# Routing and expert rows tile by tile in a two-block transformer kernel on one core

## The reference

```
for i in range(2):                       # second model
    h, hc = modulate(rmsnorm(x)), modulate(rmsnorm(xc))
    q, k, v = split(h @ w_qkv[i]); qc, kc, vc = split(hc @ w_qkv[i])
    x = x + gt_a * (attention @ w_o[i])          # xc likewise, in layer 0 only
    tokens = [modulate(rmsnorm(x)); modulate(rmsnorm(xc))]   # layer 1: x only
    # router: one of 4 groups, then the top 2 of its 8 experts
    y = sum over 2 experts of weight * (silu(t @ w_gate[e]) * (t @ w_up[e])) @ w_down[e]
    x = x + gt_f * y                             # xc likewise, in layer 0 only
return rmsnorm(x) * g_final
```

## Time and profile before

| | us |
|---|---|
| median of 3 runs | 2907.42 |
| lowest, highest | 2905.54, 2912.68 |
| the profiled execution, whole | 2902.2 |
| its span, first to last instruction | 2900.4 |
| PE busy | 2263.7 |
| VectorE busy | 1755.8 |
| ScalarE busy | 1186.0 |
| GpSimd busy | 333.8 |

### The profile page before, as it was taken

One profiled execution on the slowest core, in us unless ns is written; L12 is line 12 of the kernel. 1 busy time (PEld: TensorE's weight loads), 2 busy tenths in 40 slices (PEclk: granted clock), 3 DMA queues, 4 the chain that ended last, 5 costly groups with the idle time before them and its releaser, 6 DMA issues. The chain is left out here.

```text
span 2900.4 us, 30924 instructions
## 1 busy us (share of the span) xinstructions
PE 2263.7 (78%) x11408; PEld 1676.9 (58%) x11408; DVE 1755.8 (61%) x2142; ACT 1186.0 (41%) x1399; POOL 333.8 (12%) x431
## 2 busy tenths in 40 slices
PE   6779789996788998967737888888266648888884
PEld 5557677785576776844535555555154535555552
DVE  4646545534565445277436877777557448878785
ACT  3223234323233342234115665656223236666662
POOL 1100000100000001000022211111110121311111
PEclk9779899987798998978858999999687869999997
DMA  9235364541463645410057999999710169999993
GB/s 316 74 134 204 133 204 167 206 176 59 149 232 131 203 167 196 123 25 1 17 205 304 401 408 412 403 412 374 235 40 1 60 246 407 409 420 406 411 415 153
DMA packets 176641, 655.44 MB, mean 226 GB/s; under 512 B 18192, under 2 KB 63840, under 8 KB 151200
## 3 DMA queue, kind: packets, MB, share of 16 engines
q1 hardware_dynamic: 157008, 612.13, 55.4%
q0 software_dynamic: 18288, 38.72, 4.1%
q10 hardware_dynamic: 1248, 3.25, 0.3%
HBM read 653.70 MB, written 21.31 MB: 233 GB/s over the span
## 5 line engine op out<-in xcount | busy, mean ns | idle before, releaser
L555 PE MATMUL bank<-sb_ring_rounded,sb_hT_rounded 128*128 128x512 f32 x2864 | 768.9, 404 | 37.2 <-DVE sb_st L1458 11.3
L555 PEld LDWEIGHTS bank<-sb_ring_rounded,sb_hT_rounded 128*128 128x128 f32 x2864 | 555.5, 196 | 162.2 <-issue 12.9
L1492 DVE TENSOR_TENSOR sb_ring_rounded<-sb_ring,sb_ring_rounded 128x2048 fp32r<-128x2048 f32 (+1 forms) x150 | 332.8, 2260 | 240.9 <-ACT sb_ring_rounded L1108 240.6
L1002 PE MATMUL bank<-sb_ring_rounded,sb_arena_rounded 128*128 128x512 f32 x1024 | 429.9, 420 | 0.0
L1108 ACT ACTIVATE sb_ring_rounded<-sb_ring 128x2048 fp32r<-128x2048 f32 (+1 forms) x150 | 275.3, 1884 | 327.5 <-PE bank L555 144.0
L2043 DVE TENSOR_TENSOR sb_ring_rounded<-sb_ring,sb_hT_rounded 128x2048 fp32r<-128x2048 f32 x128 | 287.6, 2288 | 166.8 <-ACT sb_hT_rounded L1368 165.1
L1002 PE MATMUL bank<-sb_hT_rounded,sb_arena_rounded 128*128 128x512 f32 x512 | 237.6, 464 | 141.2 <-DVE sb_arena_rounded L2047 141.2
L555 PE MATMUL bank<-sb_ring_rounded,sb_arena_rounded 128*128 128x512 f32 x976 | 299.9, 395 | 2.0 <-DVE sb_arena_rounded L1480 1.0
L1002 PEld LDWEIGHTS bank<-sb_hT_rounded,sb_arena_rounded 128*128 128x128 f32 x512 | 115.0, 225 | 219.9 <-issue 178.3
L1368 ACT ACTIVATE sb_hT_rounded<-sb_ring 128x2048 fp32r<-128x2048 f32 x128 | 236.8, 1897 | 7.4 <-DMA sb_ring<-in_w_gate 7.1
L1002 PEld LDWEIGHTS bank<-sb_ring_rounded,sb_arena_rounded 128*128 128x128 f32 x1024 | 210.7, 206 | 44.1
(11 more groups left out here) (292 smaller groups left out, 2907.9 us busy)
## 6 DMA issues: line engine op xcount, KB each, us to landing
sb_ring<-in_w_gate SPq DMA_DIRECT2D x64, 2048.0 KB, 14.1
sb_ring<-in_w_up SPq DMA_DIRECT2D x64, 2048.0 KB, 18.9
sb_ring<-in_w_down SPq DMA_DIRECT2D x64, 2048.0 KB, 20.5
sb_ring<-in_w_ada SPq DMA_DIRECT2D x48, 1024.0 KB, 8.7
sb_ring<-in_ffn_w_gu SPq DMA_DIRECT2D x44, 1024.0 KB, 7.9
sb_ring<-in_xa_w_kv SPq DMA_DIRECT2D x16, 1024.0 KB, 10.9
sb_ring<-in_ffn_w_down SPq DMA_DIRECT2D x16, 1024.0 KB, 6.3
sb_ring<-in_od_w_in SPq DMA_DIRECT2D x12, 1024.0 KB, 8.6
```

Of the source, the lines that this page charges most:

```text
L555: ins = pe.matmul(bank[b][0:rows, :], rnd(x), rnd(w[:, k, :]), start=start and k == k0 and q == 0, stop=stop and k == k1 - 1 and q == len( ...
L1002: ins = pe.matmul(bank[2 * j + part][:, :], rnd(mxT[:, j, kk, :]), rnd(w), start=kk == 0 and q == 0, stop=kk == KD - 1 and q == 1)
L1492: dve.tensor_tensor(rnd(w), w, whole(high_of(n)[:, k0:k1, :]), ALU.subtract).then_inc(*c.up(s["w_lo"]))
```

## The change

It changes the second model alone, in `joint`, `route`, `experts` and the end.

- w_o: after the left half, each tile's right half is followed at once by that tile's squares and mean, and by scale and shift of the tile before it, into a region `hr` of its own. The rows for that are broadcast into `bcx` by GpSimd from the time at which the attention's output has been split (`o_split`).
- route: PE turns the tiles and makes the logits of the tile before between them; ScalarE copies both halves out. The weights of the first experts are called at the first of these transposes (before: at the first router product).
- table: VectorE makes from each rank a block number and a place within the block, as marks: `mrow` (64 places) and `mcol` (8 blocks x 32 experts, times the assignment's number less 4096). Eight products (four in layer 1) sum them to the table in PSUM, and `idx` is that plus 4096. The table in DRAM, its scatters and loads, the PE transposes of it are gone. The eight or six small steps for the number of loop turns now come behind this.
- experts: the gathers of the first four experts take the column of `idx` directly, without the copy. SP fetches the down weights of experts 0 and 1 together at the start.
- y: SP calls it back (before: GpSimd), one semaphore per tile, in layer 0 behind the first qkv slot of layer 1. Combine and squares are done per tile. In layer 0 the context tiles 2 and 3 are combined within layer 1's `joint`, between the projections of tiles 0 and 1; they are normed and turned before the last two products of the third slot. Rows of layer 1's first norm and g_final are broadcast before the loop.
- the end: each tile is stored by itself.

```
 # SP, experts
+                    early = isinstance(i, int)
...
-                        since(sp, m["pe_y_hi"], e - 1)
-                        fetch(2, j, of(e))
+                        if early:
+                            if j == 0:
+                                fetch(2, 0, 0)
+                                fetch(2, 1, 1)
+                        else:
+                            since(sp, m["pe_y_hi"], e - 1)
+                            fetch(2, j, of(e))
...
                 sp.wait_ge(m["pe_y_hi"], steps * 2)
                 if l == 0:
-                    for q in range(2):
-                        sp.wait_ge(s[f"y_loaded{q}"], 32)
+                    load(loads_to[0])
+                sp.wait_ge(s["y_stored"], l + 1)
+                for t in range(4 - 2 * l):
+                    sp.dma_start(y_rows[:, t, :, :], DR["y"][l][2 * t * P:2 * (t + 1) * P, :].rearrange("(p j) d -> p j d", j=2)).then_inc(s[f"y_loaded{t}"], 16)
 # PE, joint of layer 1
-                    gemm(n0 + 2, 1, [0, 1, 2, 3], copy_by, LO_J)
+                    gemm(n0 + 2, 1, [0, 1], copy_by, LO_J)
+                    norm(2)
+                    hT_settled()
+                    gemm(n0 + 2, 1, [2, 3], copy_by, LO_J, 2)
 # PE, route
+                turn(0)
+                pe.wait_ge(*c.next(s["small_l"], 64))
+                for t in range(1, tiles):
+                    turn(t)
+                    logits(t - 1)
+                hT_settled()
+                logits(tiles - 1)
...
-                pe.wait_ge(*c.next(s["tab_loaded"], 64))
                 claim(S1)
-                for q in range(2):
-                    ins = pe.transpose(bank[S1][0:ROWS, q * P:(q + 1) * P], mtab[:, q, :], ident)
+                for q in range(2 * tiles):
+                    if q % tiles == 0:
+                        pe.wait_ge(*c.next(s["marks_ready"]))
+                    ins = pe.matmul(bank[S1][0:ROWS, 0:BLK * N_EXP], mrow[:, q, :], mcol[:, q, :, :], start=q == 0, stop=q == 2 * tiles - 1)
 # VectorE, joint of layer 1
+                    modulate_tiles([0, 1])
+                    turned([0, 1], LO_J)
+                    ahead(first["qkv1"])
+                    dve.wait_ge(*c.next(s["bcx"], 16))
+                    combine(2, ctx_gate)
+                    project(0, 1, 1)
+                    combine(3, ctx_gate)
+                    ahead(first["qkv1"] + 1)
+                    settle()
+                    inv_rms([2, 3])
+                    project(1, 1, 3)
+                    modulate_tiles([2, 3])
                     ahead(first["qkv1"] + 2)
+                    turned([2, 3], LO_J)
 # VectorE, after w_o
+                for t in tiles:
+                    residual(None, [(1, t)], gates=(2, 0), u0=len(tiles) + t)
+                    step(dve.tensor_tensor_reduce(hr[:, t, :], xs[:, t, :], xs[:, t, :], 1.0, 0.0, ALU.mult, ALU.add, st[:, t:t + 1]))
+                    dve.tensor_scalar(st[:, 4 + t:5 + t], st[:, t:t + 1], 1.0 / D, EPS, ALU.mult, ALU.add).then_inc(*c.up(s["ms_ready"]))
+                    if t == 0:
+                        dve.wait_ge(*c.next(s["bcx"], 16 * len(tiles)))
+                    else:
+                        scaled(t - 1)
+                scaled(len(tiles) - 1)
 # VectorE, route, behind the ranks
+                step(dve.tensor_scalar(blocks, rank, 1.0 / ROWS, None, ALU.mult))
+                step(dve.tensor_tensor(past, wide(blocks, BLK + 1), cst[:, C_IOTA:C_IOTA + BLK + 1].unsqueeze(1).to_broadcast([P, J, BLK + 1]), ALU.is_ge))
+                step(dve.tensor_reduce(whole_blocks, past, AX, ALU.add))
+                step(dve.scalar_tensor_tensor(whole_blocks, whole_blocks, -float(ROWS), rank, ALU.mult, ALU.add))
+                step(dve.tensor_tensor(mrow[:, 0:J, :], cst[:, C_ROW:C_ROW + ROWS].unsqueeze(1).to_broadcast([P, J, ROWS]), wide(whole_blocks, ROWS), ALU.is_equal))
+                step(dve.tensor_tensor(value, past[:, :, 0:BLK], past[:, :, 1:BLK + 1], ALU.subtract))
+                step(dve.tensor_tensor(value, value, wide(cst[:, C_ASG:C_ASG + J], BLK), ALU.mult))
+                for half in range(2):
+                    q = slice(half * T, (half + 1) * T)
+                    dve.tensor_tensor(mcol[:, q, :, :], value[:, q, :].unsqueeze(3).to_broadcast([P, T, BLK, N_EXP]),
+                                      hots[:, q, :].unsqueeze(2).to_broadcast([P, T, BLK, N_EXP]), ALU.mult).then_inc(*c.up(s["marks_ready"]))
 # VectorE, end of experts
+                if l == 0:
+                    split(moe_at[0])
                 filled(2)
+                for t in range(2):
+                    combine(t, bc[:, 2, :])
+                    settle()
...
+                    squares(t, t)
 # GpSimd, gather
-                pool.tensor_copy(pick[:, 0, j:j + 1], column(1, e)).then_inc(m["picked_in"], 1)
-                pool.wait_ge(m["picked_in"], e + 1)
+                if isinstance(e, int):
+                    pool.sem_inc(m["picked_in"], 1)
+                    at = column(1, e)
```

More of the change, by code:

```diff
@@ L598, in hT_settled, with gemm @@
                 claim(T1)
[L600 to L602 removed]
+            def gemm(n0, slots, tiles, reader, lo=LO2, u=0):
                 for i in range(slots):
@@ L944, in route, with turn, logits @@
             def route(l, tiles):
-                norm(2, split=False)
-                if tiles == 4:
-                    norm(2, split=False)
-                hT_settled()
-                pe.wait_ge(*c.next(s["small_l"], 64))
-                for t in range(tiles):
+                def turn(t):
+                    pe.wait_ge(*c.next(s["h_ready"]))
+                    for half in range(2):
+                        b = (T0, T1)[half]
+                        claim(b)
+                        for k in range(4):
+                            ins = pe.transpose(bank[b][:, k * P:(k + 1) * P], hr[:, t, (4 * half + k) * P:(4 * half + k + 1) * P], ident)
+                            if t == 0 and half == 0 and k == 0:
+                                using(ins, uses_to[l])
+                        publish(ins, b, "a")
+                def logits(t):
                     claim(t)
@@ L2316, in _ @@
                 tiles = 4 - 2 * l
-                pool.wait_ge(s["ms_ready"], c.count(s["ms_ready"]) + 1)
-                fill(0, mod(l, 0, 4))
-                fill(1, mod(l, 0, 3))
-                norms()
-                fill(2, mod(l, 0, 5))
+                pool.wait_ge(*c.next(s["o_split"]))
+                for q in range(tiles):
+                    pool.dma_start(bcx[:, q, :], mod(l, q // 2, 4 - q % 2).partition_broadcast(P)).then_inc(s["bcx"], 16)
                 with nc.allow_non_contiguous_dma(reason="router's narrow weights"):
```

194 lines of the change are left out of this document (103 added, 91 removed).

## The result

Median 2813.0 us (2809.4 to 2813.8, 4 runs) against 2906.5 (2900.2 to 2912.7, 4 runs) for the kernel before on the same chip: ratio 0.9676, 95% interval 0.9653 to 0.9699. The forecast was 2812, range 2793 to 2832. The profiled execution of after took 2809.4 with a span of 2807.6; the sum of the prediction gave 2807 for it.

The account below looks back on a forecast made before the run. DMA paces the expert loops, untouched; engines waiting in line bound the four gaps around them. Gains 39 + 0 + 26 + 21.6 + 8 = 95 us off 2902.2 give 2807, with 5 for the median 2812; range 2793 to 2832.

Parts of the forecast that it names:

- A1: Layer 0, w_o to router logits: norming tile by tile brings the logits read from 1482.27 to 1461, gain 21 us.
- the cover: Layer 0 w_o: VectorE's 5.4 us of norm work per tile fits the 5.44 us between products, with nothing spare.
- A2: Layer 0, ranks to idx: building the table by products takes 8.3 us instead of 24.3, gain 16.
- the halving of 0.228: Table products: time per record of products twice as wide, 0.228, halved to 0.11 at high clock; 0.27 taken.
- A3: Layer 0, idx to first expert product: gathering without GpSimd's column copy gains 2.3 us.
- the three cases: First gather beside VectorE's split: slips in ahead, 4.4 us; held to that split's end, 2.3; held through both, 0.
- Down weights early: Expert loops: fetching expert 1's down weights early costed at 0, bounds 0 to 10 us for both layers.
- B: Loop 0's end into layer 1: combine and norm between qkv products, first product 32.4 us sooner, net gain 26.
- C: Layer 1 routing, last w_o read to first expert product: gain 21.6 us, with the gather taking 9.3 to land.
- Rival 1: Gather, token store and y share queues with weights called sooner: 2830 us; chance 0.12.
- D: Kernel's end: tile 0 lands alone, g_final lies ready, half the output store off the end; gain 8 us.
- rival 3: Expert loops fall to the low clock each turn; at 1.7 us more per expert 2921, slower; chance 0.03.

## Why the prediction was right

**A1** (21, measured 22.9). Right in place: the cover held. VectorE shows no idle at the last w_o read, and the reads of the tiles stand 5.44, 5.37 and 5.44 us apart as before. The logits were read at 1460.71 for 1461. The clock's part has the size that the two ends of the text allow (1456.5 and 1462.3): at the high level the last 32 router products would have given 3.2 more, as in the run with the norm behind the last product.

**A2** (16, measured 15.0). The table's products took 5.01 us for 16, 0.31 each, for the 0.27 taken and above the 0.3 named as the most; idx came 9.4 after the ranks instead of 8.3. The step that was mis-sized is the halving of 0.228. In the trace of after the records of those wider products (L1057) begin in pairs, one for each half of the columns, as at 2007.06 and 2007.09 and again at 2007.48 and 2007.52: 0.43 us for two, so 0.228 is a mean of records that run side by side. The table's records run one by one. They begin 0.43 us apart until the granted clock rises at 1480.4 (1477.61, 1478.06, 1478.49) and 0.215 apart behind that (1481.17, 1481.38, 1481.60), where the text had 0.3 at the most and 0.11. Put back, the old table costs 20 because of the prefetch, so what the products save in this kernel is more than the difference of the two traces. The margin in layer 0 was smaller than the text has it: the weights were in at about 1482 and not 1476, 1.6 us before idx, since 3.1 MB of token stores and broadcast rows share the queues with their 12.6 MB.

**A3** (2.3, measured 2.2). Right, and by the stated mechanism: dropping the copy drops one hold of two. The middle of the three cases was the true one, and the hold that stays is worth 1.3 more.

**Down weights early** (0). Right for the loops, as far as their scatter lets one see. The step missed that the fetch stands ahead of layer 1's gather: -3.7 there, part of C.

**B** (26, measured 24.6). The first qkv product came 31.0 nearer to the loop's end for 32.4: y was called at 7.7 us after the loop and not 6.7, since the last store took 6.0 to land beside the qkv load (2.5 at the end of the kernel; the text gave it 2 extra). The pause was 4.6 for 6.2, as the transposes ran at the high level (1.03 and 1.16 us). "Just in time" was right: VectorE's list fills the time up to 2077.6 and PE turns at 2077.67. To the end of the qkv products the gain is 26.4 (85.3 us after the loop against 111.8), and 1.8 is lost after them, where the low level lasted 47.8 us against 44.4 before.

**C** (21.6, measured 19.2). Logits 7.1 for 6.7. Ranks to idx 7.05 for 5.5, gain 15.4 for 17: all eight records of the table's products ran at the low level and took 3.64 us, where 0.27 each makes 2.2. That is the halving again, and nearly all of the miss. Idx to first product 14.1, for 13. Rival 1, the prefetch in the way, is at work in this stage, with 5.6 us by the run with both down weights late, but the sum had it already as 9.3 against 2.6.

**D** (8, measured 5.0). y landed and was scaled 3.2 sooner (3.6 forecast). g_final is gone: squares to final scale 2.9 for 5.6, as "4 less 1.4". The step that failed is "half of the output store and two flag copies are off the end": that would give 1.8 and it cost 1.0, as GpSimd's DRAIN, begun with the last power, ends 3.0 us behind the stores' landing. Before, the same instruction began at 2890.0 with the last power and ended at 2899.0, 1.2 us before the store had landed. With the power moved away the tail fell by 3.0.

**The loops** (0, measured 4.8) are no gain of the change as far as the runs show: loop 0 ranges from 515.2 to 518.5 with the same code. So the sum came out 2 us from the truth, with 3 lost in D, 2.4 in C and 1.4 in B, 1.4 ahead of A, won back by 1.5 in A and 4.8 in loops that happened to be short. The mechanisms are right; that the total is this close is luck, as is the median's 1 us, since five executions of the same kernel lay between 2801.4 and 2820.6.

Two sums of the prediction don't come out, and nothing hangs on them. The ends given for the stages add up to 79 and 125, not 80 and 119. And rival 3's 2825 + 96 should be the forecast and 1.7 us for each of 64 turns, 2812 + 109; the result, 2921, stays.

## What to carry to other kernels

Count a prefetch against everything that needs the same queues soon after it, not only against what it feeds: here the early weights would make a table in DRAM 4 to 5 us dearer, and held layer 1's gather for 5.6 us, 3.7 of them by one fetch that brought nothing. When work leaves a tail, ask of every engine when it gives its last instruction: the end was set by one that had nothing to do with the output. And compare a stage between traces only at the same granted clock; traces of the same code whose level differed stood up to 7.5 us apart at the end of B, as much as many of the terms. Last, a mean time per record of a group says nothing of one record where two run side by side.

## What the runs showed of the hardware

- Each engine ends with a DRAIN. GpSimd's is long, and the execution does not end before it: 9.0 us before (from 2890.0), 8.5 after (from 2798.9), both begun with its last instruction, and 6.9 where its last power was moved away, with the end 3.0 us sooner. The kernels open their block with `no_gpsimd_drain=False`; what the end costs without that is not on record.
- An indirect DMA's instruction on GpSimd, 1.03 us alone, is held by a VectorE operation with two SBUF inputs to its end and then takes 0.9: 2.28 or 3.0 us. The VectorE operation is not held.
- A signal sent from GpSimd's queue behind such an instruction left before it (the split that waited for it began at 1480.32, the instruction at 1480.50).
- A record of a float32 product with 256 columns (128*64, 128x256) takes 0.43 us at the low level and 0.215 at the high one.
- The same code runs at different granted clocks in different executions. In ten traces whose code here is after's, the mean granted clock over the 15 us from 36 us behind the first qkv product was 1.00 three times, 0.89 three times and 0.77 four times. The last w_o read followed the loop by 222.4 to 222.7, by 224.1 to 226.8 and by 226.6 to 229.9 us. (One of them, 224.1, has another order of VectorE's list around w_o.) What decides between the levels, the runs don't show.
